# Block sums by accumulating DMA and earlier token blocks in a seven-product feedforward

## The reference, cut to what matters

```python
def swiglu(h, wg, wu, wd):
    return (jax.nn.silu(h @ wg) * (h @ wu)) @ wd
...
h = rmsnorm(x, g[0])
x = x + 0.5 * rmsnorm(swiglu(h, ffn_wg[l, 0], ffn_wu[l, 0], ffn_wd[l, 0]), g[1])
```

## Time and profile before

| | |
|---|---|
| median of three runs | 1484.91 us |
| profiled execution, its time and its span | 1485.87 us, 1484.1 us |
| TensorE busy | 1383.7 us, 93% |
| VectorE busy | 1101.7 us, 74% |
| ScalarE busy | 819.8 us, 55% |
| GpSimd busy | 80.3 us, 5% |
| DMA, mean over the span | 185 GB/s |

### The profile page before, as it was taken

The page is one execution under the profiler, slowest core; times in us unless marked ns, Lnnn a source line. Parts: engine busy times, 40 slices in busy tenths (PEclk is TensorE's granted clock), DMA queues, the critical chain, the costliest instruction groups (busy, mean ns, idle before and its releaser), DMA issues. The chain is left out here.

```text
span 1484.1 us, 19388 instructions
## 1 busy us (share of the span) xinstructions
PE 1383.7 (93%) x6943; PEld 1145.2 (77%) x6943; DVE 1101.7 (74%) x1565; ACT 819.8 (55%) x1301; POOL 80.3 (5%) x133
## 2 busy tenths in 40 slices
PE   5999999999995999999895999987999999959998
PEld 4878877999974888887674888866888877848886
DVE  6577786989778887479969887579785546698863
ACT  4547746655545555366655555455464567655552
POOL 3011100000000000031100000000000100000000
PEclk8999999999997999999997999997999999989999
DMA  9887654676542747353262847426575473438460
GB/s 353 287 285 232 216 170 146 209 272 230 198 156 85 255 129 266 120 184 114 86 213 85 257 144 252 150 92 224 172 236 189 126 221 115 156 100 269 143 226 29
DMA packets 160702, 274.37 MB, mean 185 GB/s; under 512 B 5953, under 2 KB 87617, under 8 KB 160609
## 3 DMA queue, kind: packets, MB, share of 16 engines
q1 hardware_dynamic: 153904, 250.86, 50.7%
q0 software_dynamic: 5552, 20.20, 4.4%
q10 hardware_dynamic: 1153, 2.07, 0.4%
HBM read 272.05 MB, written 1.06 MB: 184 GB/s over the span
## 5 line engine op out<-in xcount | busy, mean ns | idle before, releaser
L2327 DVE TENSOR_TENSOR w_lo<-raw,w_hi 128x1024 fp32r<-128x1024 f32 (+1 forms) x312 | 370.8, 1231 | 78.4 <-ACT w_hi L2065 77.5
L2065 ACT ACTIVATE w_hi<-raw 128x1024 fp32r<-128x1024 f32 (+1 forms) x312 | 309.8, 1047 | 102.6 <-PE psum L2801 54.4
L2799 PE MATMUL psum<-w_hi,hT_hi 128*128 128x512 f32 x760 | 307.1, 404 | 6.3 <-DVE hT_lo L2493 3.7
L2800 PE MATMUL psum<-w_lo,hT_hi 128*128 128x512 f32 x760 | 298.0, 392 | 0.0
L2801 PE MATMUL psum<-w_hi,hT_lo 128*128 128x512 f32 x760 | 297.9, 392 | 0.0
L2799 PEld LDWEIGHTS psum<-w_hi,hT_hi 128*128 128x128 f32 x760 | 144.2, 190 | 40.5 <-issue 10.0
L2801 PEld LDWEIGHTS psum<-w_hi,hT_lo 128*128 128x128 f32 x760 | 144.2, 190 | 31.2
L2800 PEld LDWEIGHTS psum<-w_lo,hT_hi 128*128 128x128 f32 x760 | 144.5, 190 | 27.8 <-issue 0.6
L2799 PE MATMUL psum<-w_hi,hc_hi 128*128 128x512 f32 x256 | 101.2, 395 | 0.7 <-DVE hc_lo L2718 0.6
L2801 PE MATMUL psum<-w_hi,hc_lo 128*128 128x512 f32 x256 | 99.9, 390 | 0.0
L2800 PE MATMUL psum<-w_lo,hc_hi 128*128 128x512 f32 x256 | 99.8, 390 | 0.0
(11 more groups left out here) (301 smaller groups left out, 2831.8 us busy)
## 6 DMA issues: line engine op xcount, KB each, us to landing
raw<-in_ffn_wd_dram SPq DMA_DIRECT2D x44, 1024.0 KB, 5.0
raw<-in_ffn_wg_dram SPq DMA_DIRECT2D x56, 512.0 KB, 4.0
raw<-in_ffn_wu_dram SPq DMA_DIRECT2D x56, 512.0 KB, 5.3
raw<-in_w_up_dram SPq DMA_DIRECT2D x44, 512.0 KB, 5.1
raw<-in_w_in_dram SPq DMA_DIRECT2D x19, 1024.0 KB, 7.7
raw<-in_ffn_wg_dram SPq DMA_DIRECT2D x16, 1024.0 KB, 5.2
raw<-in_ffn_wu_dram SPq DMA_DIRECT2D x16, 1024.0 KB, 5.2
ada_raw<-in_w_ada_dram POOLq DMA_DIRECT2D x24, 512.0 KB, 5.4
```

Of the source, the lines that this page charges most:

```text
L2065: nc.scalar.activation(hi_of(s)[:, cs], source_of(s)[:, cs], ACT.Copy).then_inc(ready, 1)
L2327: nc.vector.tensor_tensor(lo_of(u)[:, cs], source_of(u)[:, cs], hi_of(u)[:, cs].bitcast(F32), ALU.subtract)\
L2799: nc.tensor.matmul(o, a_hi, b_hi, start=start, stop=False)
L2800: nc.tensor.matmul(o, a_hi, b_lo, start=False, stop=False)
```

## The change

1. The sums of three and four are no longer formed by VectorE. GpSimd issues a DMA that adds a weight block from HBM onto `blended` in place (`accum_op=ALU.add`), once the unit last made from `blended` is split. It adds up4 onto gate0+up0 for u6, and gate4 onto that for u4. ScalarE's split of u6 and u4 waits for the landing (`sum_landed`).
2. Signs are changed so that all weight sums are plain sums: the token sums, `gsum`, `gup` and the last gate step subtract where they added and the reverse.
3. The order of the units is u1, u5, u7, u2, u6, down, u3, u4.
4. The mixed token blocks are made sooner: rows and sums around the row statistics, the high part behind the first chunk's gate evacuation, the low part behind the next unit's split. Before, all of it came behind the second chunk's evacuation, and the low part behind the splits for down unit 0.
5. The up gate product of token tile 0 moves from the step of u2 to that of u3.

```diff
@@ sum_unit
+        if isinstance(b, int):
+            self.formed[u] = dict(by="vector", no=self.n_formed, dst=dst, a=a, b=b, last=last)
+        else:
+            self.formed[u] = dict(by="dma", no=self.n_landed, dst=dst, src=b, last=last)
@@ go_on
             if not self.conv:
+                pl.add("token_rows", g=self.G[KT - 1, 1])
                 self.st = x_stats(x_at)
+                pl.add("token_sums")
             self.mm(0, 1)
             self.mm(1, 1)
             self.out(0)
+            if not self.conv:
+                pl.add("token_high")
             pl.split_to(us[3] + 1)
+            if not self.conv:
+                pl.add("token_low")
             self.mm(2, 1)
             self.hidden_turn(0)
...
-            pl.add("mixed_rows", g=self.G[KT - 1, 1])
             self.down(0)
-            pl.add("mixed_split")
@@ group
             u5 = pl.sum_unit(block(up, 0), "sums", "own", u1)
-            u7 = pl.sum_unit(block(up, 4), u5, "own", u5)
-            u6 = pl.sum_unit(None, "sums", u7, "sums")
+            u7 = pl.sum_unit(block(up, 4), u5, u5, "own")
+            u2 = pl.unit(4, BANK, [(0, BANK, block(gate, 4))])
+            u6 = pl.sum_unit(None, "sums", "sums", block(up, 4))
...
             product_of(u7, p7, True, tile=None, mixed=2)
             pl.add("gkeep", use=p5, slot=1)
+            p2 = pl.use(banks[0], u2)
+            product_of(u2, p2, False, tile=(4, 0), mixed=None)
+            pl.add("ggate", t=0, use=p2, stat=self.st, n=n)
+            p6 = pl.use(banks[3], u6)
             product_of(u6, p6, True, tile=None, mixed=0)
             pl.add("gsum", kept=(p1, p5), uses=(p6, p7), n=n)
             self.down(c - 1)
...
-            u4 = pl.sum_unit(None, "sums", u2, "sums")
-            pl.release[u2] = u4
+            u4 = pl.sum_unit(None, "sums", "sums", block(gate, 4))
@@ gpsimd
+                elif kind == "split_hi":
+                    made = plan.formed.get(a["unit"])
+                    if made is not None and made["by"] == "dma":
+                        pool.wait_ge(hi_ready, made["last"] + 1)
+                        pool.wait_ge(lo_ready, made["last"] + 1)
+                        pool.dma_start(blended.rearrange("p (k n) -> p k n", k=4), made["src"], accum_op=ALU.add)\
+                            .then_inc(sum_landed, 16)
@@ scalar, split_hi
+                    elif made is not None:
+                        act.wait_ge(sum_landed, 16 * (made["no"] + 1))
@@ vector, gsum and gup (their last operations)
-                    nc.vector.tensor_tensor(kept[:, 1, :], kept[:, 0, :], kept[:, 1, :], ALU.add).then_inc(group_summed, 1)
+                    nc.vector.scalar_tensor_tensor(kept[:, 1, :], kept[:, 1, :], -1.0, kept[:, 0, :], ALU.mult, ALU.subtract)                        .then_inc(group_summed, 1)
-                    nc.vector.tensor_tensor(kept[:, 2, :], psum[:, use.bank, :], kept[:, 0, :], ALU.add)\
+                    nc.vector.scalar_tensor_tensor(kept[:, 2, :], psum[:, use.bank, :], -1.0, kept[:, 0, :], ALU.mult,
```

More of the change, by code:

```diff
@@ L147, in __init__ @@
         self.n_group, self.last_sum = 0, None
+        self.n_formed, self.n_landed = 0, 0
         self.stat_cols = 0
@@ L161, in sum_unit @@
         u = self.unit(4, BANK, [(0, BANK, load)] if load is not None else [])
-        a, b = (u if v == "own" else v for v in (a, b))
-        self.formed[u] = dict(no=len(self.formed), dst=dst, a=a, b=b, last=self.last_sum if dst == "sums" else None)
+        a, b = (u if isinstance(v, str) and v == "own" else v for v in (a, b))
+        last = self.last_sum if dst == "sums" else None
+        if isinstance(b, int):
+            self.formed[u] = dict(by="vector", no=self.n_formed, dst=dst, a=a, b=b, last=last)
+            self.n_formed += 1
+        else:
+            self.formed[u] = dict(by="dma", no=self.n_landed, dst=dst, src=b, last=last)
+            self.n_landed += 1
         if dst == "sums":
@@ L946, in group @@
             product_of(u3, p3, False, tile=None, mixed=1)
[L947 to L951, removed]
-            u4 = pl.sum_unit(None, "sums", u2, "sums")
-            pl.release[u2] = u4
+            pl.add("gup", use=p3, gate=p2, stat=self.st, n=n)
+            u4 = pl.sum_unit(None, "sums", "sums", block(gate, 4))
             p4 = pl.use(banks[2], u4)
@@ L2062, in split_hi @@
                     cs = half_of(s, half)
-                    if made is not None:
+                    if made is not None and made["by"] == "vector":
                         act.wait_ge(sum_ready, 2 * made["no"] + half + 1)
+                    elif made is not None:
+                        act.wait_ge(sum_landed, 16 * (made["no"] + 1))
                     nc.scalar.activation(hi_of(s)[:, cs], source_of(s)[:, cs], ACT.Copy).then_inc(ready, 1)
@@ L2300, in form @@
             def form(u):
-                if u not in plan.formed or u in formed:
+                if u not in plan.formed or u in formed or plan.formed[u]["by"] == "dma":
                     return
@@ L2307, in form @@
                 for v in (made["a"], made["b"]):
-                    if v != "sums" and v not in plan.formed or v == u:
+                    if v != "sums" and (v not in plan.formed or v == u or ("w", v) in raw_slot):
                         dve.wait_ge(weight_loaded[raw_slot["w", v]], landed["w", v])
[L2310 to L2313, removed]
+                if made["last"] is not None:
+                    dve.wait_ge(hi_ready, made["last"] + 1)
+                    dve.wait_ge(lo_ready, made["last"] + 1)
                 if made["no"]:
                     dve.wait_ge(sum_ready, 2 * made["no"])
-                plus, minus = raw_of(made["a"]), blended if made["b"] == "sums" else raw_of(made["b"])
+                a, b = (blended if v == "sums" else raw_of(v) for v in (made["a"], made["b"]))
                 for half in range(2):
                     cs = half_of(u, half)
-                    nc.vector.tensor_tensor(source_of(u)[:, cs], plus[:, cs], minus[:, cs], ALU.subtract).then_inc(sum_ready, 1)
+                    nc.vector.tensor_tensor(source_of(u)[:, cs], a[:, cs], b[:, cs], ALU.add).then_inc(sum_ready, 1)
             def split_lo_half(u, half):
@@ L2367, in _ @@
                     n_mixed[0] += 1
+                elif kind == "token_sums":
                     base = 6 * n_mixed[0] - 6
@@ L3028, in _ @@
                         .then_inc(psum_ready[use.bank], 1)
-                elif kind == "mixed_rows":
+                elif kind == "token_low":
                     n_mixed[0] += 1
```

51 lines of the change are left out of this document (23 added, 28 removed).

## The result

| | before | after |
|---|---|---|
| median | 1485.56 us (4 runs) | 1547.96 us (1542.16 to 1549.14, 4 runs) |
| ratio, 95% interval | | 1.0414 (1.0385 to 1.0443) |
| span of the profiled execution | 1484.1 us | 1547.4 us |
| TensorE busy / idle | 1383.7 / 100.4 us | 1418.8 / 128.6 us |

The account below looks back on a forecast made before the run. TensorE was taken as the bound, losing time only where it stands still. Four feedforwards losing 2.8 + 1.5 us add 17 us to 1485.87: 1503, median 1502, called 1500 as some low clock loss may vanish; range 1490 to 1515.

Parts of the forecast that it names:

- the first chain: Landing, u6's and down's high splits, copy of p1 (4.6 us), then u2's product and TensorE's work to E: T5 + L + 22.7.
- T5: First group: the moment VectorE ends u5's low split and loads and first accumulation start; 1316.9 us, 1318.1 before.
- L: Time from T5 to the landing of the first accumulation, for u6; taken as 14 us.
- the wait for `hc_lo`: A new wait of TensorE ahead of down product 0, 4.2 us, four times.
- An accumulation's price of two copies: An accumulating DMA of 1 MB takes all 16 engines 6.7 us, against 3.35 us for a copy.
- VectorE's relief: Two sums fewer in each of eight groups take 38 us off VectorE, but from where TensorE doesn't wait for it.
- the low clock: Slow matmuls after a long wait: 1.7 us charged after the wait ahead of u2's product in the first group.
- E: The moment TensorE starts the next single chunk behind a group; before, 1350.80 us in the first and 1415.59 in the second.
- the first group: In each feedforward, the group whose E was forecast at 1353.6 us against 1350.8 before: 2.8 us lost.
- The second group: In each feedforward, the group whose E was forecast at 1417.1 us against 1415.6: 1.5 us lost, 11.4 us of landing hidden.
- Rival 1: The accumulation costs no more than a copy, L = 8.5 us: faster, 1471 us; chance 0.25.
- Rival 3: A slow accumulation, 3 copies or 10 us of the engines, L = 18 us: 1569 us; chance 0.24.

Follow-up runs that it names:

- e4: Changed kernel with `gup` moved directly behind `gsum`, ahead of two low splits of the next chunk; 1516.86 us.
- e1: Kernel before with only the mixed token blocks made sooner; 1462.23 us.
- e3: Changed kernel with the two accumulating DMAs of each group as plain copies, without adding; 1502.88 us.
- e5: Changed kernel with VectorE forming the sums for u6 and u4 again, so no accumulating DMA; 1509.40 us.
- e7: e4 with `gsum` also moved, directly behind u6's product, ahead of the next chunk's first split; 1545.22 us.
- e8: Changed kernel with the second hidden turn's products on bank 7; 1548.43 us.
- e9: Changed kernel with VectorE forming the sums for u6 and u4 and with `gup` directly behind `gsum`; 1481.97 us.
- e10: Kernel before with token blocks sooner, the low token part behind `hc_lo` and the second hidden turn on bank 7, rerun for its trace; 1460.45 us.

## Why the prediction was right in sign and wrong in size

**Right.** The sign, and it doesn't hang on the wait that was missed: with `gup`'s wait taken out (e4) the kernel is still 32 us slower than before. And, with 46.9 us added to the forecast moments, those of the first chain up to u2's product. T5 was forecast at 1363.8 and came at 1364.04; L at 14 us, and was 13.8 (1364.04 to 1377.84); the wait for `hc_lo` at 4.2, and was 4.20, in e1 too; u2 is held by the copy of p1, forecast at 1382.4 with the 4.6 us, and started at 1382.27. An accumulation's price of two copies holds by e3 (2.06). VectorE's relief, 37 us of the 38 forecast, shows no gain: e5 gives it back and is 39 us faster.

**Wrong: "After that TensorE does u2, u6, down, u3, u4: 16.4 us, and 1.7 us for the low clock".** That is the last link of the first chain. I treated E as a moment at which TensorE is merely done with u4. It is also a product that needs a bank: p3's, freed by `gup`. Before, `gup` came 3.8 us early, so I never asked where it stands. The new order keeps it two splits behind `gsum`, which itself moved behind the next chunk's load and split, and leaves one product in place of two between u3 and E. The rows of the order in the section on the change end at `gsum`, two splits short of `gup`. From u2's product to E it took 22.75 us, not 18.1: 3.5 for `gup` and 0.8 for `gsum`, with 0.4 left over. So the first group lost 7.3 us instead of 2.8. The second group, where u6's landing is hidden as I had said, lost 7.3 instead of 1.5, by the same `gup` (3.5), `gsum` (1.7) and the low clock behind the first E (1.7). With the 1.7 us of low clock behind the second E, 4 x 16.3 = 65 us, against 62 measured. e4 takes `gup`'s part away alone: 31 us.

The DMA's own 39 us split as E does: in e5 it is 44.1 us from down product 0 to the first E, and 50.6 in the changed kernel; from E to E 69.2, and 72.1. That is 6.5 + 2.9 = 9.4 us for each of four feedforwards, 38 us.

**Mis-sized: the low clock.** I charged it once in each feedforward, to the long wait ahead of u2's product, which only takes the place of the charge of before, and took 2 us off the sum on the ground that it may vanish in shorter waits. It is the reverse: nearly every wait of 3 us or more paid the same 1.7 us as the one of 15.7 us, and in the fourth feedforward the change made five out of one. That is some 30 us of the 62, and e7 and e8 show it from both sides.

**Missed, with no effect on the time.** u7's wait of 6.5 us. I had u7 end at 1321.4, or 1368.3 with the 46.9 us, and a single wait of some 13 us behind it ahead of u2; u7 started at 1374.17, and u2 waited 2.98 us. u7's bank is the one that `hidden_turn(1)` uses, whose `hc_lo` stands behind u2's low split, and that waits for u2's load. By e8 it hides beside the first chain.

**Rival 1** took 8.5 us for a landing at a copy's price. e3 landed in 8.4, but made 1503, not 1471: its E still had the wait for `gup` (21.0 us in all).

**Rival 3**, the slow accumulation, comes nearer to the time than the forecast does, with 1569, and is wrong all the same: it took 18 us for the first landing and 15 for the second, and they took 13.8 (from T5) and 8.8.

What stays open: what part of e9's 20 us over e1 is due to the product order, and what to the changed signs and the moved gate step. No run separates them.

## What to carry to other kernels

When an order changes, list for the next product behind the changed stretch everything it needs, its PSUM bank too, and follow each reader of that bank through its own engine's new queue, even where it was early before. Price a wait of TensorE as its length plus the slow matmuls behind it: with 1.7 us for each, an estimate from the stages above, three waits of 3 us cost 14.1 us and one of 9 us 10.7. No run here compares just these. And count a removed wait as won only if the chain that ends beside it goes too.

## What the runs showed of the hardware

- A DMA that adds into SBUF took 2.06 times the engine time of the same DMA as a copy (5.9 and 2.9 us of all 16 engines for 1 MB), and it landed 3 to 5 us later (13.2 and 8.8 us, against 8.4 and 5.5). GpSimd was at its issue for 1.3 us, and for 0.8 us at the copy's.
- In the changed kernel's fourth feedforward, waits of TensorE of 3.0, 3.5, 4.2 and 6.5 us were each followed by 5 to 7 us with a granted clock of 0.61 to 0.76; in e7, two waits of 2.60 and 0.97 us, with 1.8 us of work between them, were too (0.54). A single 0.91 us and a pair of 0.15 and 1.27 us in e4 were not.
- The length of a wait alone doesn't tell. The 3.49 us in the changed kernel's third feedforward was followed by 1.00. In e10 the wait ahead of down product 0, 1.8 to 2.0 us, was followed by 0.72 over 6 us in three feedforwards and by 1.00 in the fourth.
